# FFN up-projection: seven block products of halves in three passes over the rows, with weight operands kept in device memory

## What is computed

```python
D_MODEL = 1024; SEQ = 2048; DEC_SEQ = 64; D_FF = 2816; FFN_CONV = 3

def causal_dwconv(x, prev, w, b):
    k_width = w.shape[0]
    L = x.shape[1]
    xp = jnp.concatenate([prev.astype(x.dtype), x], axis=1)
    y = b.astype(x.dtype) + w[0] * xp[:, 0:L]
    for j in range(1, k_width):
        y = y + w[j] * xp[:, j:j + L]
    return y, xp[:, L:]

    up, ffn_conv_state = causal_dwconv(x @ ffn_w_in, ffn_conv_prev, ffn_conv_w, ffn_conv_b)
    gate, val = split_cols(up, (D_FF, D_FF))
    x = layer_norm(DN_ALPHA * x + (jax.nn.silu(gate) * val) @ ffn_w_out, ln2_g, ln2_b)
```

## Time and profile before

| | us |
|---|---|
| median of 3 runs | 2884.21 |
| lowest, highest | 2882.98, 2893.74 |
| span of the profiled execution | 2884.9 |
| PE busy in it | 2676.0 |
| DVE, ACT, POOL busy | 1303.1, 835.6, 321.3 |

### The profile page before, as it was taken

One profiled execution on the slowest core, in us unless ns is written; L12 is line 12 of the kernel. 1 busy time (PEld: TensorE's weight loads), 2 busy tenths in 40 slices (PEclk: granted clock), 3 DMA queues, 4 the chain that ended last, 5 costly groups with the idle time before them and its releaser, 6 DMA issues. The chain is left out here.

```text
span 2884.9 us, 43107 instructions
## 1 busy us (share of the span) xinstructions
PE 2676.0 (93%) x14830; PEld 2441.9 (85%) x14830; DVE 1303.1 (45%) x2763; ACT 835.6 (29%) x1585; POOL 321.3 (11%) x351
## 2 busy tenths in 40 slices
PE   6999799948997969997999999999999979999998
PEld 5887799947986858877999999999999968888885
DVE  5342554525775857665333333333333334333323
ACT  4543322215652232224222222222222223111111
POOL 0000100001001740110111111111111100000000
PEclk9999899978997979998999999999999989999999
DMA  5443632158433554435111111111111135232321
GB/s 194 148 148 107 205 113 92 62 60 184 113 101 85 179 179 147 167 120 175 47 45 45 58 36 53 39 50 42 47 44 44 45 124 172 79 92 76 93 78 50
DMA packets 281406, 283.73 MB, mean 98 GB/s; under 512 B 35708, under 2 KB 248836, under 8 KB 281306
## 3 DMA queue, kind: packets, MB, share of 16 engines
q1 hardware_dynamic: 267866, 233.88, 27.3%
q0 software_dynamic: 13456, 48.76, 5.1%
HBM read 174.06 MB, written 109.46 MB: 98 GB/s over the span
## 5 line engine op out<-in xcount | busy, mean ns | idle before, releaser
L99 PE MATMUL fu_ps_y<-fu_xt_hi,fu_w_hi 128*128 128x426 f32 (+1 forms) x1760 | 626.1, 356 | 10.8 <-DVE fu_xt_lo L1926 8.2
L101 PE MATMUL fu_ps_y<-fu_xt_hi,fu_w_lo 128*128 128x426 f32 (+1 forms) x1760 | 626.8, 356 | 0.0
L100 PE MATMUL fu_ps_y<-fu_xt_lo,fu_w_hi 128*128 128x426 f32 (+1 forms) x1760 | 625.9, 356 | 0.0
L99 PEld LDWEIGHTS fu_ps_y<-fu_xt_hi,fu_w_hi 128*128 128x128 f32 x1760 | 331.7, 188 | 21.5 <-issue 11.7
L1960 DVE SCALAR_TENSOR_TENSOR fu_conv<-fu_ps_y,fu_vecs,fu_conv 128x424 f32<-128x424 f32 (+1 forms) x220 | 141.4, 643 | 458.8 <-ACT fu_conv L1897 458.8
L100 PEld LDWEIGHTS fu_ps_y<-fu_xt_lo,fu_w_hi 128*128 128x128 f32 x1760 | 332.0, 189 | 10.2
L101 PEld LDWEIGHTS fu_ps_y<-fu_xt_hi,fu_w_lo 128*128 128x128 f32 x1760 | 331.2, 188 | 9.0
L99 PE MATMUL fd_ps_y<-fd_w_hi,fd_h_hi 128*128 128x512 f32 (+1 forms) x748 | 292.7, 391 | 14.4 <-DVE fd_h_lo L2159 14.3
L100 PE MATMUL fd_ps_y<-fd_w_lo,fd_h_hi 128*128 128x512 f32 (+1 forms) x748 | 292.0, 390 | 0.0
L101 PE MATMUL fd_ps_y<-fd_w_hi,fd_h_lo 128*128 128x512 f32 (+1 forms) x748 | 291.8, 390 | 0.0
L1897 ACT ACTIVATE fu_conv<-fu_ps_y,fu_vecs 128x424 f32<-128x424 f32 (+1 forms) x220 | 153.3, 697 | 426.8 <-PE fu_ps_y L101 346.6
(11 more groups left out here) (281 smaller groups left out, 4177.2 us busy)
## 6 DMA issues: line engine op xcount, KB each, us to landing
fu_w_raw<-ffn_w_in SPq DMA_DIRECT2D x44, 512.0 KB, 4.4
fd_h_raw<-h_t SPq DMA_DIRECT2D x176, 128.0 KB, 2.1
h_t<-fu_h SPq DMA_DIRECT2D x88, 212.0 KB, 2.0
fd_raw<-ffn_w_out SPq DMA_DIRECT2D x22, 512.0 KB, 4.5
x_rows<-pr_xr SPq DMA_DIRECT2D x16, 512.0 KB, 2.8
xt<-pr_xt SPq DMA_DIRECT2D x16, 512.0 KB, 4.0
mo_mx<-mixed SPq DMA_DIRECT2D x16, 512.0 KB, 4.4
mo_x<-x_rows SPq DMA_DIRECT2D x16, 512.0 KB, 3.3
```

The source lines that it names most:

```text
L99: pe.matmul(out, lhs_hi, rhs_hi, start=first, stop=False)
L100: pe.matmul(out, lhs_hi, rhs_lo, start=False, stop=False)
L101: return pe.matmul(out, lhs_lo, rhs_hi, start=False, stop=last)
```

## The change

Only `ffn_up` changes. Its product becomes 2 x 2 blocks: the weights of a unit j are A11, A12 (the gate tile's lower and upper half of the 1024 input features) and A21, A22 (the value tile's); the rows of a pass are two halves, and B11, B21 (first half of the rows, lower and upper features), B12, B22 (second half) are their blocks. The four blocks C11, C12 (gate) and C21, C22 (value) come from seven products instead of eight, with the sums S1 = A21 + A22, S2 = S1 - A11, S3 = A11 - A21, S4 = A12 - S2 and T1 = B12 - B11, T2 = B22 - T1, T3 = B22 - B12, T4 = B21 - T2. The products are made in the order 1 (A11 B11), 2 (A12 B21), 6 (S2 T2), 5 (S1 T1), 7 (S3 T3), 3 (S4 B22), 4 (A22 T4), which is also the number of their slot; a product has 4 blocks of 128 features x 3. Some of them accumulate on each other in PSUM, after ScalarE has copied out the partial result that is needed alone.

There are NQ = 3 passes over the rows, of 2 x 352, 2 x 352 and 2 x 354 columns (354 and 356 with the two rows in front), and 22 units (pairs of a gate and a value tile) in each: 66 units. The second half of the last pass holds the end of the prompt, two columns for the state, and the sample rows, so the sample rows need no taps of their own. In pass 0 VectorE and ScalarE make the 7 weight operands with their hi and lo parts for the next unit, and SP stores them in a new tensor `w_split` (`store_w`); in passes 1 and 2 SP loads them (`load_w`), each slot as soon as its product of two units before is done. The seven x operands of a pass are made by `differences` (VectorE), `split_x_hi` and `split_x_lo`; for the next pass this happens in the last two units of a pass, where `turn` is set. The copy of `vecs` now stands behind ScalarE's first casts.

```diff
-        GW = 424
-        NG = -(-ROWS // GW)
-        REST = SEQ - (NG - 1) * GW
-        LASTW = REST + NSMP
-        U = 2 * NG
+        NQ = 3
+        PW = 704
+        KH = KD // 2
...
+        ORDER = (1, 2, 6, 5, 7, 3, 4)
+        SLOT = {p: i for i, p in enumerate(ORDER)}
+        X_B11, X_B21, X_T2, X_T1, X_T3, X_B22, X_T4 = range(7)
+        W_A11, W_A12, W_S2, W_S1, W_S3, W_S4, W_A22 = range(7)
+        CHUNK_OF = (0, 0, 1, 1, 2, 2, 3)
+        CHUNKS = [slice(W_A11, W_A12 + 1), slice(W_S2, W_S1 + 1), slice(W_S3, W_S4 + 1), slice(W_A22, W_A22 + 1)]
...
+        x_hi, x_lo = m.sb("x_hi", [P, 7, KH, WX], F32R), m.sb("x_lo", [P, 7, KH, WX], F32R)
+        w_raw = m.sb("w_raw", [P, 2, 2, KD, P])
+        w_at = m.here()
+        w = m.sb("w", [P, 2, 7, 2, KH, P], F32R)
+        w_hi, w_lo = w[:, :, :, 0], w[:, :, :, 1]
+        w_sum = m.over("w_sum", w_at, [P, 2, 7, 2, KH, P])[:, :, :, 1]
+        w_split = nc.dram_tensor("fu_w_split", (KF, 7, P, 2 * KH * P), F32, kind="Internal").ap()
...
+        def units(eng, body):
+
+            for q in range(NQ):
+                body(q, 0, 0)
+                body(q, 1, 1)
+                with eng.Fori(1, KF // 2 - 1) as i:
+                    body(q, 2 * i, 0)
+                    body(q, 2 * i + 1, 1)
+                body(q, KF - 2, 0)
+                body(q, KF - 1, 1)
...
+                def store_w(j, p, chunk):
+                    sp.wait_ge(w_lo_done, 4 * j + chunk + 1)
+                    alone(sp)
+                    s = CHUNKS[chunk]
+                    sp.dma_start(split_rows(j, s), w[:, p, s].bitcast(F32).rearrange("p s h k c -> p s (h k c)")).then_inc(w_stored[p], 16)
+
+                def load_w(q, j, p, slot):
+
+                    sp.wait_ge(mm_done, 7 * (KF * q + j - 2) + slot + 1)
+                    alone(sp)
+                    sp.dma_start(w[:, p, slot:slot + 1].bitcast(F32).rearrange("p s h k c -> p s (h k c)"),
+                                 split_rows(j, slice(slot, slot + 1))).then_inc(w_loaded[p][slot], 16)
+
+                for chunk in range(4):
+                    store_w(0, 0, chunk)
+
+                def body(q, j, p):
+                    nxt2 = ahead(q, j, 2)
+                    last_two = isinstance(j, int) and j >= KF - 2
+                    if q == 0 and not last_two:
+                        sp.wait_ge(w_lo_done, 4 * j + 4)
+                        sp.wait_ge(s_done, 4 * j + 4)
                         alone(sp)
-                        load_w(j + 1, half)
-                    for g in range(NG):
-                        sp.wait_ge(h_done, NG * j + g + 1)
-                        alone(sp)
-                        k = slice(j, j + 1) if isinstance(j, int) else bass.ds(j, 1)
-                        sp.dma_start(d["h_t"][:, k, g * GW:g * GW + gwidth(g)].rearrange("p a c -> p (a c)"),
-                                     h[:, g % 2, :gwidth(g)]).then_inc(h_stored[g % 2], 16)
-                pairs(sp, step)
-                sp.wait_ge(h_stored[0], 16 * stored_before(KF, 0))
-                sp.wait_ge(h_stored[1], 16 * stored_before(KF, 1))
+                        load_raw(*nxt2, p)
+                    if q == 0 and last_two:
+                        sp.wait_ge(w_stored[p], 64 * (KF // 2))
+                    for i in range(7):
+                        if i == (2 if q else 0) and not is_first(q, j):
+                            store_h(*before(q, j))
+                        if q == 0 and i < 4 and not (isinstance(j, int) and j == KF - 1):
+                            store_w(j + 1, 1 - p, i)
+                        if nxt2 and nxt2[0] >= 1:
+                            load_w(*nxt2, p, i)
+                    if isinstance(j, int) and j == 1 and q + 1 < NQ:
+                        sp.wait_ge(x_lo_done, 7 * (q + 1))
...
+                split_hi(0, 0, 0)
+                for slot in range(2):
+                    split_x_hi(0, slot)
+                split_hi(0, 0, 1)
+                split_x_hi(0, 2)
+                split_x_hi(0, 3)
+                split_hi(0, 0, 2)
+                split_x_hi(0, 4)
+                split_x_hi(0, 5)
+                split_hi(0, 0, 3)
+                split_x_hi(0, 6)
                 act.wait_ge(vec_turned, 1)
-                act.copy(vecs[:].rearrange("p a b -> p (a b)"), ps_y[:, 0, 0:6 * MT]).then_inc(vec_done, 1)
+                act.copy(vecs[:].rearrange("p a b -> p (a b)"), ps_v[:, 0:6 * MT]).then_inc(vec_done, 1)
                 act.wait_ge(vec_done, 1)
...
+                def sums(j, p, steps):
+
+                    a11, a12, a21, a22 = (w_raw[:, p, half, ks, :] for half in range(2) for ks in (slice(0, KH), slice(KH, KD)))
+                    s1, s2, s3, s4 = (w_sum[:, p, s] for s in (W_S1, W_S2, W_S3, W_S4))
+                    if 0 in steps:
+                        dve.wait_ge(raw_loaded[p], raws(j, p))
+                        wait_if(dve, mm_done, 7 * (j - 1))
+                        if not (isinstance(j, int) and j < 2):
+                            dve.wait_ge(w_stored[p], stores(j, p))
+                        dve.tensor_tensor(s1, a21, a22, ALU.add).then_inc(s_done, 1)
+                        dve.wait_ge(s_done, 4 * j + 1)
+                        dve.tensor_tensor(s2, s1, a11, ALU.subtract).then_inc(s_done, 1)
+                        dve.wait_ge(s_done, 4 * j + 2)
+                        dve.tensor_tensor(s4, a12, s2, ALU.subtract).then_inc(s_done, 1)
+                    if 1 in steps:
+                        dve.tensor_tensor(s3, a11, a21, ALU.subtract).then_inc(s_done, 1)
...
+                def body(q, j, p):
+                    u = KF * q + j
...
+                    nxt = ahead(q, j, 1)
+                    turn = isinstance(j, int) and j == KF - 1 and q + 1 < NQ
+                    if not is_first(q, j):
+                        b = before(q, j)
+                        nb = width(b[0])
+                        taps(*b, 3, gate1[:, :nb], c12)
+                        taps(*b, 4, val0[:, :nb], ps_a[:, 1 - p])
+                    if turn:
+                        for step in differences(dve, q + 1)[2:]:
+                            step()
+                    if isinstance(j, int) and j == KF - 2 and q + 1 < NQ:
+                        for step in differences(dve, q + 1)[:2]:
+                            step()
+                    split = nxt and nxt[0] == 0
+                    if split:
+                        sums(nxt[1], 1 - p, (0,))
+                        split_lo(nxt[1], 1 - p, 0)
+                    dve.wait_ge(mm_done, 7 * u + 2)
+                    dve.wait_ge(copy_done, 3 * u + 1)
+                    dve.tensor_tensor(c11[:, :w], p1[:, :w], ps_b[:, p, :w], ALU.add).then_inc(add_done, 1)
+                    if turn:
+                        split_x_lo(q + 1, 0)
+                        split_x_lo(q + 1, 1)
+                    if split:
+                        sums(nxt[1], 1 - p, (1,))
+                    taps(q, j, 1, gate0[:, p, :n], c11)
+                    if split:
+                        split_lo(nxt[1], 1 - p, 1)
+                    dve.wait_ge(mm_done, 7 * u + 5)
+                    dve.wait_ge(copy_done, 3 * u + 3)
+                    dve.tensor_tensor(c22[:, :w], p5[:, :w], ps_a[:, p, :w], ALU.add).then_inc(add_done, 1)
+                    if q == NQ - 1:
+                        sample_state(q, j, 2, c22, j + KF)
+                    if turn:
+                        split_x_lo(q + 1, 2)
+                    if split:
+                        split_lo(nxt[1], 1 - p, 2)
+                    dve.wait_ge(mm_done, 7 * u + 6)
+                    dve.tensor_tensor(c12[:, :w], u2[:, :w], ps_c[:, p, :w], ALU.add).then_inc(add_done, 1)
+                    if q == NQ - 1:
+                        sample_state(q, j, 3, c12, j)
+                    taps(q, j, 2, val1[:, :n], c22)
+                    if split:
+                        split_lo(nxt[1], 1 - p, 3)
+                    if turn:
+                        for slot in range(3, 7):
...
+                def product(q, j, p, which, bank, first):
+
+                    slot = SLOT[which]
+                    n = H + width(q)
+                    if q == 0:
+                        pe.wait_ge(w_lo_done, 4 * j + CHUNK_OF[slot] + 1)
+                    else:
+                        pe.wait_ge(w_loaded[p][slot], 8 * (KF * (q - 1) + j - p) + 16)
+                    if isinstance(j, int) and j == 0:
+                        pe.wait_ge(x_lo_done, 7 * q + slot + 1)
+                    out = bank[:, p, :n]
+                    for k in range(KH):
+                        wh, wl, xh, xl = w_hi[:, p, slot, k, :], w_lo[:, p, slot, k, :], x_hi[:, slot, k, :n], x_lo[:, slot, k, :n]
+                        pe.matmul(out, wh, xh, start=first and k == 0, stop=False, skip_group_check=True)
+                        pe.matmul(out, wh, xl, start=False, stop=False, skip_group_check=True)
```

(18 more changed lines are left out.)

495 lines of the change are left out of this document (305 added, 190 removed).

## The result

The changed kernel takes 2811.18 us, the median of 4 runs (2810.52 to 2812.41), against 2884.3 for the kernel before in the same session: ratio 0.9743, 95% interval 0.9727 to 0.9759. That is 2.6% faster, 13 us more than the 2798 forecast and inside its range.

A forecast was written before the change was run, and what follows sets the result against it. TensorE, busy 93%, was taken as the bound. Matmuls 899.8, pass 0 18, turns 6 and lower clock 2 make 925.8 us; with 14.6 of later start 940.4 against 1026.6, 86 less: 2798 us, range 2764 to 2852.

The forecast's parts named there:

- case 1: The forecast itself: TensorE bounds passes 1 and 2, pass 0 within 15.2 us a unit; 2764 to 2816 us, chance 0.55.
- Matmuls: ffn_up's three passes: 5544 matmuls, 0.162 us apart at 354 columns, 13.6 us a unit, 899.8 us in all.
- case 5: Distance between matmuls does not fall with the columns, as each still loads 128 x 128 weights; 2974 us, chance 0.01.
- Pass 0: First pass: 14.4 us a unit from VectorE and DMA together, 18 us more than TensorE alone, bounds 0 and 46.
- The sum for VectorE: VectorE's instructions in a unit of pass 0, priced and summed: 13.3 to 14.3 us, 13.9 likely.
- DMA: Transfers: 373 GB/s at 13.6 us a unit in pass 0; 296 GB/s in passes 1 and 2, cost 0 if loads overlap.
- case 4: Weight loads of passes 1 and 2 come too late, at 259 GB/s; 202 us more, 3000 us, chance 0.11.
- case 2: Pass 0 bound by VectorE or the stores, 15.2 to 17 us a unit; 2816 to 2852 us, chance 0.21.
- bound of 324 GB/s: DMA rate at a full share in the down projection; at it a unit of pass 0 takes 15.7 us.
- Turns: Last units of passes 0 and 1 also carry x splits and differences: 3 us each, 6 for both (2 to 14).
- Lower clock: TensorE at a lower clock at the stage's start: 2 us.
- Start: First product later, as ScalarE copies the vector table behind its first casts and TensorE waits: 14.6 us (10 to 20).

The follow-up runs named there:

- the kernel with 8 columns: Changed kernel with GpSimd multiplying 8 of 352 columns of each h tile in pass 0, the rest of the gate product left out: 2804.29 us, ratio 0.9717.

## Why the prediction held, term by term

The forecast's mechanism was right, in case 1 of its rivals. Its sum was 925.8 us of products and 14.6 of start; measured were 942.9 and 16.1 (28.3 from first issue to first product, 12.2 before). That is 18.6 too little; the unchanged stages ahead ended 6.6 earlier in the profiled execution than in that of the kernel before, which leaves 12 of the 13 us of difference in the whole time. So the whole time came out nearer than the stage by luck. The 17.1 of the products:

- **Matmuls**: forecast 899.8; 44 units of 13.68 and 22 of 13.65 are 902.2. Off by 2.4. The distance between matmuls did fall with the columns, to 0.163 (case 5 out).
- **Pass 0**: forecast 14.4 a unit, measured 14.37. Over TensorE's pace it costs 0.69 x 22 = 15.2 us, with what the matmuls' term already carries 17 for the 18 forecast. The size is right, and half of its reason: I put it on "VectorE and DMA together". The runs put it on VectorE alone, and give the piece that I had not priced: GpSimd's two products stretch two sums by 0.3 to 0.6 us each. Without that VectorE's list fits under TensorE's 13.68. That 14.4 met 14.37 is partly luck: my likely value for VectorE by itself was 13.9, the DMA's share of the rest was nothing, and the stretched sums filled its place. The sum for VectorE (13.3 to 14.3) took its instructions as if they ran alone. The Trainium skill has this rule in "SBUF — State Buffer" (Who interferes with whom): a VectorE instruction with two inputs in SBUF contends with a GpSimd one that reads SBUF, and one with at most one such input, outside its two-port modes, doesn't. This case agrees: the sums, both inputs in SBUF, take up to 1.19 for 0.69; the taps of C21, with one input in PSUM, keep 0.58 beside the same products. The trace of the kernel before showed it, too. There GpSimd's product of 424 columns took 1.10 us, but 1.85 where it began 0.3 us behind VectorE's split of 1024 elements, and the mean of 1.28 in the earlier trace rows hides the two values (GpSimd's rows; the split began at 1815.43):

```profile
1815.77 1.85 POOL L1844 TENSOR_TENSOR fu_h<-fu_conv,fu_gate 128x424 f32<-128x424 f32 x1 [25.15 <-DVE fu_conv L1963]
1820.13 1.10 POOL L1844 TENSOR_TENSOR fu_h<-fu_conv,fu_gate 128x424 f32<-128x424 f32 x1 [2.51 <-DVE fu_conv L1963]
```

- **DMA** (case 4, and the worry in case 2): 372 GB/s with no wait of TensorE, and no change of pace at 163. The prediction's bound of 324 GB/s was demand, not a limit, and 372 over 100 us also stands above the 358 that the prediction took from the Trainium skill, "DMA: Bandwidth & Descriptors" (Specifications); the measurement decides.
- **Turns**: forecast 6, measured 11.2 over the ordinary unit: 3.6 in unit 20, 5.5 in 22, 0.6 in 42 and 1.5 in 44. The step that failed is that I priced one pair of differences, in the last unit, and left out the other: the first two of the four run in the unit before, where VectorE makes weights as well and had, by my own sum, nothing to spare. They take 2.21 and 2.12 us there beside GpSimd's product, not the 1.6 of a difference alone. At unit 22, 2.8 us are ScalarE's wait for an h store, which I had left out.
- **Not in the forecast**: the x blocks of the next pass in SyncE's queue ahead of h stores and raw weights, 7.1 us in unit 3 and 5.6 in unit 25, 12.6 together and the largest miss. I counted SyncE's queue for an ordinary unit of passes 1 and 2 only, as nine issues of 0.4 us and free. There it holds (0.33 to 0.36 us each); it left out the x blocks, and pass 0, where the raw weights' issues take 1.15 us each and the first h store's 2.0. Behind the burst these were 1.9 and 4.0, and 3.1, and everything behind them was late. Of the 5.6 us in unit 25 a part may belong to one execution, as said above.
- **Lower clock**: 2 forecast; units 0 and 1 are 1.9 over 14.37, with a granted clock of 0.52 in the first 5 us and 1.00 behind them.
- **Start**: 14.6 forecast, 16.1 measured: VectorE's differences began when the last x block was there, 15.0 us behind the first issue, where I had it at 12.6. That the start comes from the copy of the vectors behind ScalarE's casts was right as a reading and of no use as a lever: with the copy first, the same time is waited inside unit 0.

2.4 - 3.1 (pass 0, with unit 21 a little short) + 5.2 + 12.6 is 17.1.

## What to carry to other kernels

- When an engine is filled to the last 5%, lay out what runs beside it on the engine with which it contends, and price its instructions with that neighbour, not alone. A mean over two durations (1.10 and 1.85 us here) can hide that they contend.
- Walk each queue through the units that differ (first, second, last of a pass), not the ordinary one: the bursts ahead of two small stores cost up to 12.6 us here, nearly what VectorE's shortage cost in a whole pass (15.2), and another engine's queue for those stores took most of it away.
- Before moving an instruction ahead of a copy that TensorE waits for, ask what it waits for in the units at the turns: 7 us won in pass 0 were paid for with 11 in two units.

## What the chip showed that I had not expected

- 354 GB/s at a DMA share of 1.04 and 372 at 1.06 in the same loop, the latter with TensorE never waiting: a share of 1 in the windows did not mean that the transfers were the bound.
- The contention costs GpSimd too, at times by about the whole of VectorE's instruction. In the kernel with 8 columns a product took 0.20 us, but 1.57 and 1.52 where it began 0.1 to 0.2 us behind a difference of 1.6 us on VectorE. In the changed kernel two full products beside differences took 2.20 and 2.35 us (most of pass 1's take 0.94), and three differences beside such products 2.12 to 2.26. The rows are GpSimd's and VectorE's in the kernel with 8 columns:

```profile
1619.46 1.57 POOL L1959 TENSOR_TENSOR fu_val<-fu_val,fu_gate 128x8 f32<-128x8 f32 x1 [12.97 <-DVE fu_val L2158]
1620.99 0.20 POOL L1961 TENSOR_TENSOR fu_val<-fu_val,fu_gate 128x8 f32<-128x8 f32 x1
```

```profile
1619.35 1.62 DVE L1933 TENSOR_TENSOR fu_xb<-fu_xb 128x1416 f32<-128x1416 f32 x1
```

- An issue on SyncE's queue took 0.33 us in pass 1 and 0.36 to 2.0 us (medians by line) in pass 0, where the DMA share is over 1; two of 512 KB behind four of 708 KB took 6.1 us.
